# Second feed-forward block of an encoder step: half products one pair of units earlier, and the token sums moved to the front of it

## The reference, cut to what matters

```python
def swiglu(h, w_gate, w_up, w_down):
    return (jax.nn.silu(h @ w_gate) * (h @ w_up)) @ w_down
...
    x = x + 0.5 * gt3[:, None, :] * swiglu(modulate(rms_norm(x, norm_ffn2), sh3, sc3),
                                            ffn2_w_gate, ffn2_w_up, ffn2_w_down)
```

## Time and profile before

| What | Value |
|---|---|
| Median of 3 runs | 1564.29 us (1563.79 to 1565.09) |
| The profiled execution, its own time | 1563.67 us |
| Its span | 1562.0 us |
| Mean granted clock of PE | 0.979 of full |
| PE busy | 1475.0 us, 94% |
| DVE, ACT, POOL busy | 49%, 35%, 19% |

### The profile page before, as it was taken

How to read it: one execution, slowest core, us unless ns; L and a number is a source line. 1 busy time by engine, 2 the same in 40 slices (tenths; PEclk the granted TensorE clock), 3 DMA queues, 4 the chain that set the end, 5 groups by cost and what they waited for, 6 DMA issues and landing times. The chain is left out here.

```text
span 1562.0 us, 28989 instructions
## 1 busy us (share of the span) xinstructions
PE 1475.0 (94%) x11646; PEld 1381.7 (88%) x11646; DVE 765.3 (49%) x1399; ACT 539.8 (35%) x992; POOL 292.7 (19%) x300
## 2 busy tenths in 40 slices
PE   5899999999999989999997899989899999999996
PEld 3799999999999889998896667779799999999995
DVE  2532332222322452466657665573557548754763
ACT  3533112221122342554323433542544124422434
POOL 1300000000000232343002022203523024302400
PEclk9999999999999989999998999999899999999998
DMA  8543353444321414222102411224112402331221
GB/s 316 185 125 121 122 175 122 124 134 159 124 79 56 149 33 112 68 76 54 55 14 64 95 39 51 75 70 122 34 48 84 120 28 82 105 112 32 86 87 68
DMA packets 204424, 148.55 MB, mean 95 GB/s; under 512 B 17947, under 2 KB 190268, under 8 KB 204312
## 3 DMA queue, kind: packets, MB, share of 16 engines
q1 hardware_dynamic: 191352, 99.79, 22.8%
q0 software_dynamic: 12960, 47.18, 8.9%
HBM read 139.99 MB, written 6.95 MB: 94 GB/s over the span
## 5 line engine op out<-in xcount | busy, mean ns | idle before, releaser
L3052 PE MATMUL pair<-h_hi,w_hi 128*128 128x320 f32 (+1 forms) x1216 | 281.9, 313 | 2.2 <-DVEq L486 1.2
L3052 PE MATMUL pair<-h_hi,w_lo 128*128 128x320 f32 (+1 forms) x1216 | 277.8, 310 | 0.0
L3052 PE MATMUL pair<-h_lo,w_hi 128*128 128x320 f32 (+1 forms) x1216 | 277.7, 310 | 0.0
L3052 PEld LDWEIGHTS pair<-h_hi,w_hi 128*128 128x128 f32 (+1 forms) x1216 | 202.6, 188 | 15.5 <-issue 12.2
L344 DVE TENSOR_TENSOR w_lo<-w_raw,w_hi 128x1024 fp32r<-128x1024 f32 x94 | 115.1, 1226 | 184.4 <-ACT w_hi L339 179.3
L3052 PEld LDWEIGHTS pair<-h_lo,w_hi 128*128 128x128 f32 (+1 forms) x1216 | 203.8, 188 | 0.0
L3052 PEld LDWEIGHTS pair<-h_hi,w_lo 128*128 128x128 f32 (+1 forms) x1216 | 203.7, 188 | 0.0
L339 ACT ACTIVATE w_hi<-w_raw 128x1024 fp32r<-128x1024 f32 x106 | 111.4, 1053 | 164.1 <-PE pair L3052 87.6
L476 DVE SCALAR_TENSOR_TENSOR x_t<-pair,gate,x_t 128x320 f32<-128x320 f32 (+1 forms) x112 | 49.0, 479 | 197.3 <-PE pair L3052 90.9
L3165 PE MATMUL pair<-b_hi,w_hi 128*128 128x320 f32 x360 | 111.2, 309 | 0.0
L3165 PE MATMUL pair<-b_lo,w_hi 128*128 128x320 f32 x360 | 111.2, 309 | 0.0
(11 more groups left out here) (438 smaller groups left out, 2880.2 us busy)
## 6 DMA issues: line engine op xcount, KB each, us to landing
w_mod_raw<-w_mod POOLq DMA_DIRECT2D x28, 1024.0 KB, 7.7
w_raw<-ffn_w_gate SPq DMA_DIRECT2D x42, 512.0 KB, 3.7
w_raw<-ffn_w_up SPq DMA_DIRECT2D x24, 512.0 KB, 3.8
w_raw<-ffn_w_down SPq DMA_DIRECT2D x24, 512.0 KB, 3.8
w_raw<-w_in SPq DMA_DIRECT2D x24, 512.0 KB, 3.7
raw_more<-ffn_w_up SPq DMA_DIRECT2D x20, 512.0 KB, 3.8
w_raw<-ffn_w_down SPq DMA_DIRECT2D x12, 384.0 KB, 3.4
w_mod_a<-w_mod POOLq DMA_DIRECT2D x4, 1024.0 KB, 10.9
```

What stands on the lines that cost most here:

```text
L3052: mm = pe.matmul(pair[u % 2][0:width, b, 0:HALF], w[:, 0:width], x_parts[part][:, k, b * HALF:(b + 1) * HALF], start=(k == 0 and v == 0), ...
```

## The change

`WHOLE_PAIRS` goes from 2 to 1, so that the block begins with four whole units in place of eight, and the work of the last four is done by two more jobs (now called jobs 2 and 3; the jobs that were 4 to 21 are unchanged). `T_UNIT` goes from 3 to 0, so that the token splits stand behind units 0 to 3 and not 3 to 6. POOL makes s1 and s2 of the first job between the second and the third group of token sums.

```diff
-WHOLE_PAIRS = 2
+WHOLE_PAIRS = 1
 JOB0 = 2 * WHOLE_PAIRS
-T_UNIT = 3
+T_UNIT = 0
...
             for kk in range(KH):
+                if kk == KH // 2:
+                    part_sum(pool, JOB0, "s1")
+                    part_sum(pool, JOB0, "s2")
                 pool.wait_ge(h_lo_done, H_KEYS + 2 * kk + 2)
...
-            for j, part in SUM_ORDER:
+            for j, part in SUM_ORDER[2:]:
                 part_sum(pool, j, part)
```

## The result

The changed kernel takes 1575.24 us (median of 4 runs, 1573.76 to 1576.26), the kernel before beside it 1564.04 us (4 runs, 1561.1 to 1565.09). The ratio is 1.0074, 95% interval 1.0056 to 1.0091: slower by 0.74%, some 11.6 us. The prediction was +12.0, 1576 us.

What follows compares the result with a forecast made beforehand. PE's matmuls were taken to bound the second feed-forward block. Waits less saved matmuls made the next job +9.7 us late; 2.3 for the clock gave +12.0, on the 1564.29 us median 1576.3, given as 1576, range 1569.5 to 1580.5.

Steps and rivals of the forecast that it cites:

- Fewer matmuls: On PE, 192 matmuls of units 4 to 7 go and 168 of jobs 2 and 3 come: 3.5 us gained.
- First wait: Ahead of unit 3, PE waits 2.1 us for DVE's multiplication of unit 1, queued behind token splits, a11 and s2.
- The joint work: POOL's sums and DVE's splits from 1123.15 us to the third group's last token split add to 21.6 us, ending at 1144.8.
- The price list in turns: POOL and DVE alternate at SBUF: token sum 0.74, weight sum 1.13, token split 0.38, half-weight split 0.55, row split 0.68 us.
- no idle time: Sign in the changed profile: POOL never idle between 1123 and 1145 us, with sums at 1.1 to 1.9 us.
- The last chain: From unit 3's multiplication through row copy and fourth group's token splits to PE's first half product: 4.06 us, impossible to hide.
- The clock: Behind the 11 us gap PE runs 16 to 23 matmuls at half clock, costing 1.9 to 2.6 us, taken as 2.3.
- Taking the first wait as too short for the clock: The 2.1 us wait ahead of unit 3 was costed at no clock loss (bounds 0 and 2.0).
- the long wait: Ahead of the first half product, PE waits 11.1 us after unit 3 for the last token splits, starting at 1150.2.
- The sum: Whole kernel: 9.7 us for the block plus 2.3 for the clock make +12.0 us, 1576.3 on the median.
- The rival with little contention: POOL and DVE mostly miss each other at SBUF: block +2.2, clock 1.9, total 1568.4 us; chance 0.15.
- nothing on PE behind the first half product waits: What follows job 3 keeps its instructions, places and cover, so it was costed at nothing.

Runs made afterwards that it cites:

- units8_t4: Kernel before, eight whole units, with T_UNIT 4 in place of 3, so the fourth group's token splits stand behind the last unit's activation; 1570.89 us, ratio 1.0047.
- tokens_first: Changed kernel with ACT and DVE splitting the fourth token group before unit 3's activation, s3 and s4 after it; 1574.25 us, ratio 1.0050.
- fill_gap: Changed kernel with 72 matmuls of unused result run on PE ahead of its wait for the token splits; 1576.84 us, ratio 1.0073.
- hold_job3: Changed kernel with POOL's s1 and s2 of job 3 held until DVE has split the third group of token sums; 1579.69 us, ratio 1.0083.
- reorder_early: Changed kernel with ACT's and DVE's order turned round, PE waiting by token group, first job's s1 and s2 made before the modulation; 1564.03 us, ratio 0.9989.
- tuned: reorder_early with POOL's s1 of job 3 held until DVE has split s4 of job 2; 1561.48 us, ratio 0.9987.

## Why the prediction was right

**Fewer matmuls (-3.5 us).** The profile has 24 weight loads fewer, and the busy window from 1175 us on has 0.146 us a matmul, as before.

**First wait (2.1 us).** Unit 3 started at 1129.75, 2.09 us behind 1120.61 + 7.05. The multiplication stood behind the splits as forecast, at 1128.74, 8.1 us behind unit 2's start against 8.2 in the forecast.

**The joint work (to 22.0 us behind unit 2's start).** The third group's splits ended at 1142.63, 22.0 us behind. The price list in turns held. One sign did not: POOL stood still for 1.0 us at s3, which waits for DVE's split of s1, where I had said that it would have no idle time. It cost nothing, since DVE worked on splits that the sum counts anyway.

**The last chain (4.06 us).** From the multiplication at 1143.75 to PE at 1147.90 it is 4.15. units8_t4 measures it alone, 4.3 us. That these 4.06 us "cannot be hidden by anything" holds for this order only: in tokens_first most of them leave the path.

**The clock (2.3 us).** 21 matmuls at 0.50 are 2.5 us, and fill_gap gives 2.65. Taking the first wait as too short for the clock rested on one row, and was luck: it was right in the changed kernel's profile, but in hold_job3, fill_gap and tokens_first the clock fell behind it too (15 matmuls in 3.7 us in hold_job3). It cost nothing in hold_job3 and tokens_first, since the long wait took it up; in fill_gap it came back as 1.05 us.

**The sum.** Start to start, +2.1 and +11.1 for the waits, +2.5 for the clock, -3.5 for the matmuls: +12.2, where the block has +12.3 and the timed runs 11.6. The agreement to a few tenths is closer than the reading of prices from single rows could promise. The rival with little contention, +4.1, failed at the token splits of 5.15 and 5.97 us. That nothing on PE behind the first half product waits was right also.

**What blurs the timed runs.** The block starts anywhere from 1101.6 to 1110.3 us in these profiles, behind the same matmuls. The granted clock of that first part differs from one execution to the next, in one place above all. Before, and in hold_job3:

```profile
936.00:960.00 24.00, 21.48 (x353) 16.75 (x352) 13.25 (x39) 7.47 (x21) 7.99 (x13) 0.93 0.32 95
```

```profile
936.00:960.00 24.00, 21.45 (x286) 15.95 (x282) 12.34 (x37) 5.12 (x14) 8.95 (x14) 0.76 0.33 95
```

Between its 6500th and its 7000th matmul, around this place, hold_job3 goes from 1.4 us ahead of the kernel before to 4.1 us behind it. The four profiles whose block starts latest (1106.7 us and later) have 0.76 to 0.83 in this window, the changed kernel has 0.95. The timed runs go the same way: of 35 of the kernel before in the last group, the six with a mean clock of 0.974 or less took 1566.8 to 1570.8 us, the ten with 0.979 or more 1561.2 to 1563.8. Why the clock is granted differently in executions of the same instructions stays open. It moves the timed medians by as much as the last experiments do.

## What to carry to other kernels

Ahead of taking work off the bounding engine, ask what that work covered: here 28 us of matmuls hid token sums, and a saving of 3.5 us laid open a wait of 11. Read the side chain in queue order on each engine, and where GpSimd and VectorE both read two SBUF tensors, as here in float32, add their durations. What helped here was an order that puts the needed piece first (3.5 us) and idle time far ahead (2.4 us); holding the other engine back gave 1.1 us of 2.3 once and nothing once. Put a wait at the first instruction that needs it, and activations whose result is not due behind those that are.

## What the runs showed that I had not expected

The clock fell behind a wait of 1.9 us in three of four profiles with that wait, and a slowed stretch of PE just ahead of a longer wait was free in hold_job3 and tokens_first; in fill_gap, where PE had 72 matmuls to run in that wait, it came back as 1.05 us. Turns are strict: a split of 512 columns that takes 0.68 us alone took 1.36 us beside token sums (1126.18 in the changed kernel, POOL's from 1125.87 on) and 1.6 to 1.8 us beside weight sums (hold_job3, reorder_early, tuned). And a sum that was held until a later point met the next splits, both times that it was tried.
